# A two-block fp32 model on one core: unit 0 of the second scan prepared between the value tiles of the shift projection

## What is computed

```python
cols = cols + (bidir_shift(cols) - cols) * mu          # 0.5 * (left + right neighbour)
r, k, v, w_lo, a_lo, g_lo = split(cols)                # widths 512, 512, 512, 128, 128, 128
w_log = -softplus(-(w0 + tanh(w_lo) @ w2)) - 0.5
decay = exp(-exp(w_log))
iclr = sigmoid(a0 + a_lo @ a2)
kk = l2norm(heads(k * k_k))
k_dir = heads(k * (1 + (iclr - 1) * k_a))
b_dir = kk * heads(iclr)
y = rwkv7_scan(r, decay, k_dir, v, -kk, b_dir)         # two directions, 8 heads of 64
...
y = sigmoid(g_a) * (o_a @ w_o_a) + sigmoid(g_b) * (o_b @ w_o_b)
```

## Time and profile before

| | |
|---|---|
| time of the kernel, median of 3 runs | 2380.62 us (2380.04 to 2385.37) |
| the profiled execution's own time | 2382.07 us |
| its span | 2380.3 us |
| mean granted PE clock | 0.985 |
| PE busy | 2265.9 us, 95% |
| DVE, ACT, POOL busy | 1189.4, 1003.6, 300.1 us |
| shift projection, end of its last matmul | about 1804.3 us |
| unit 0's products begin on PE | 1816.76 us |
| second half of unit 0's base begins on PE | 1821.71 us |

### The profile page before, as it was taken

How to read it: one execution, slowest core, us unless ns; L and a number is a source line. 1 busy time by engine, 2 the same in 40 slices (tenths; PEclk the granted TensorE clock), 3 DMA queues, 4 the chain that set the end, 5 groups by cost and what they waited for, 6 DMA issues and landing times.

```text
span 2380.3 us, 51755 instructions
## 1 busy us (share of the span) xinstructions
PE 2265.9 (95%) x23025; PEld 1905.8 (80%) x23025; DVE 1189.4 (50%) x2080; ACT 1003.6 (42%) x1614; POOL 300.1 (13%) x421
## 2 busy tenths in 40 slices
PE   7999999999999999999999999998999898899877
PEld 7999887889999999887889999568846787786432
DVE  5655544276655665544266655755453445432101
ACT  5434456444434444457445434643225544312111
POOL 0100000040100110000040100026312333300000
PEclk9999999999999999999999999999999999999988
DMA  8754532256655754532346762320112102087998
GB/s 269 248 204 169 169 137 101 94 179 196 228 195 177 248 204 168 199 112 102 107 159 205 244 211 88 106 73 4 42 36 72 39 8 70 8 338 278 420 421 336
DMA packets 209679, 396.61 MB, mean 167 GB/s; under 512 B 9512, under 2 KB 107613, under 8 KB 198573
## 3 DMA queue, kind: packets, MB, share of 16 engines
q1 hardware_dynamic: 207273, 388.79, 46.0%
q0 software_dynamic: 1136, 2.17, 0.3%
q10 hardware_dynamic: 1044, 2.29, 0.3%
HBM read 392.18 MB, written 1.05 MB: 165 GB/s over the span
## 4 chain that ended last, share of the span: by engine, by line
PE 85%; DVE 4%; DMA 4%; SPq 3%; ACT 2%; issue 2%; POOL 0%; ACTq 0%; DVEq 0%; POOLq 0%
PE ps L286 84%; DMA EX<-in_moe_w_up 3%; SPq L454 2%; SPq L560 1%; PE ps L1196 0%; DVE wl L487 0%; DVE AR L699 0%; ACT AR L2962 0%; ACT AR L2954 0%; DVE AR L2017 0%; PE ps L583 0%; ACT AT L1250 0%; DMA VR<-in_diff_gain 0%; DVE AR L1778 0%; ACT wh L478 0%
## 5 line engine op out<-in xcount | busy, mean ns | idle before, releaser
L487 DVE TENSOR_TENSOR wl<-RB,wh 128x2048 fp32r<-128x2048 f32 (+5 forms) x189 | 412.3, 2185 | 273.2 <-ACT wh L478 272.8
L286 PE MATMUL ps<-H,RB 128*128 128x256 f32 (+2 forms) x1728 | 452.8, 421 | 2.5 <-ACT AR L2933 1.3
L478 ACT ACTIVATE wh<-RB 128x2048 fp32r<-128x2048 f32 (+5 forms) x189 | 342.2, 1815 | 226.1 <-PE ps L286 200.0
L286 PEld LDWEIGHTS ps<-H,RB 128*128 128x128 f32 (+1 forms) x1728 | 320.2, 190 | 114.2 <-issue 76.2
L286 PE MATMUL ps<-xhf,wl 128*128 128x256 f32 x1408 | 402.3, 286 | 3.3 <-DVE xlf L728 2.4
L286 PE MATMUL ps<-xlf,wh 128*128 128x256 f32 x1408 | 398.8, 283 | 0.0
L286 PE MATMUL ps<-xhf,wh 128*128 128x256 f32 x1408 | 398.8, 283 | 0.0
L286 PE MATMUL ps<-AR 64*64 64x64 f32 (+6 forms) x8536 | 278.5, 233 | 40.3 <-issue 22.2
L286 PEld LDWEIGHTS ps<-AR 64*64 64x64 f32 (+3 forms) x8536 | 252.7, 142 | 75.3 <-issue 56.9
L286 PEld LDWEIGHTS ps<-xhf,wl 128*128 128x128 f32 x1408 | 270.6, 192 | 14.5 <-issue 9.4
L286 PEld LDWEIGHTS ps<-xlf,wh 128*128 128x128 f32 x1408 | 270.8, 192 | 0.1
(11 more groups left out here) (444 smaller groups left out, 3371.7 us busy)
## 6 DMA issues: line engine op xcount, KB each, us to landing
RB<-in_ffn_w_gu SPq DMA_DIRECT2D x88, 1024.0 KB, 7.7
RB<-in_w_in SPq DMA_DIRECT2D x23, 2048.0 KB, 8.0
RB<-in_ffn_w_down SPq DMA_DIRECT2D x16, 2048.0 KB, 7.8
RB<-in_w_gate SPq DMA_DIRECT2D x16, 2048.0 KB, 8.7
RB<-in_ada_w SPq DMA_DIRECT2D x12, 2048.0 KB, 10.1
EX<-in_moe_w_gate SPq DMA_DIRECT2D x21, 1024.0 KB, 23.3
EX<-in_moe_w_up SPq DMA_DIRECT2D x21, 1024.0 KB, 25.7
EX<-in_moe_w_down SPq DMA_DIRECT2D x9, 2048.0 KB, 25.9
```

Source lines behind the costliest of these rows:

```text
L286: return M.matmul(o, lhsT, rhs, start=start, stop=stop, skip_group_check=True)
L478: S.activation(self.pair(h)[0], of(slot_of(*key)), ACT.Copy).then_inc(*did("high", *mark))
L487: V.tensor_tensor(lo, of(slot_of(*key)), hi.bitcast(F32), ALU.subtract).then_inc(*did("low", *mark))
```

## The change

It changes seven things, all around the shift projection and the list of the scan:

- The tiles run in the order 0 to 7, 12, 13, 14, 8, 9, 10, 11 (`tiles`), and the low-rank weights are loaded ahead of the value's.
- Behind the places 10 to 13 (`early`) each engine walks the pieces of unit 0's preparation and its products. `scan_pe` and its kin take the list as an argument, and are called with `ahead(p)`.
- `PAD` and `SX` lie in a buffer of their own (`SPARE`), as their old place belongs to unit 0's preparation. The expert slot that shares this memory waits for `moved 11` instead of an earlier mark.
- Unit 0 reads the small weights straight from `EARLY`. The copies into `HB` stand behind the last tile, and POOL waits for all three (`g2`, `a2`, `w2`) before it begins the scan's list.
- From place 9 on the tiles use banks 0 to 3, the turns of the value tiles bank 4, each one place later against its tile; the last stands behind the last tile. The first branch's output is turned behind place 8.
- `merge0` 0 and 1 stand between `base_a` and `base_b` of slot -1, both in bank 4.
- `gate0` 0 moves from the old front into slot -1, 1 into its end, and 2 into slot 0. Slot -1 keeps two gates, slot 0 has gates 2 and 3; from slot 1 on the list is as before. `weigh` 0 and 1 follow them.

The core of the diff:

```diff
-        for i in range(4):
+        for i in (0, 1, 3, 2):
             job(("rkv", i), ...
...
-            order = prepared(0, 0, 1) + fill(("merge0", 0, 0)) + prepared(0, 2) + fill(*gate(0), ("merge0", 1, 0))
-            order += prepared(0, *range(3, 7)) + [(("products", 0, o),) for o in range(2)] + fill(("weigh", 0, 0))
-            sigmoid = {-1: gate(1), 3: [("merge0", 6, 0)] + gate(6)}
+            order = []
+            sigmoid = {-1: gate(0), 0: gate(2), 3: [("merge0", 6, 0)] + gate(6)}
...
-            end = {i: gate(i + 3) for i in range(-1, 3)}
+            end = {i: gate(i + 3) for i in range(3)}
+            end[-1] = gate(1)
...
-                slot = [solve(n, "base_a", 0), solve(n, "base_b", 0)] + prepared(p, 0)
+                slot = [solve(n, "base_a", 0)] + fill(*([("merge0", 0, 0), ("merge0", 1, 0)] if i < 0 else []))
+                slot += [solve(n, "base_b", 0)] + prepared(p, 0)
...
+            tiles = (*range(8), 12, 13, 14, *range(8, 12))
+            early = {10: [("prep", 0, 0)], 11: [("prep", 0, 1), ("prep", 0, 2)], 12: [("prep", 0, x) for x in (3, 4, 6)],
+                     13: [("products", 0, 0), ("products", 0, 1)]}
...
+                        ps = bank(("shift", n), ("shift_pad", n), among=every_bank if p < 9 else (0, 1, 2, 3))
...
-                    if 9 <= n < 13:
-                        vj = n - 9
+                    if p < 15:
+                        scan_pe(ahead(p))
+                    if p >= 12:
+                        vj = p - 12
                         PE.wait_ge(*at("moved", 8 + vj))
-                        ps = bank(("turned", "rv", vj), ("rv_rows", vj))
+                        ps = bank(("turned", "rv", vj), ("rv_rows", vj), among=(4,))
...
+                PO.wait_ge(*upto("low_rank"))
+                PO.wait_ge(*at("shift", 11))
+                P.tensor_copy(G2, EARLY[2]).then_inc(*did("g2"))
+                PO.wait_ge(*at("g2"))
+                PO.wait_ge(*at("a2"))
+                PO.wait_ge(*at("w2"))
```

More of the change, by code:

```diff
@@ L2529, in rwkv, with ahead @@
             BON = SM[:, 1248:1264].rearrange("p (k c) -> p k c", k=4)
-            PAD = [area(10496 + 516 * i, 516).rearrange("p (s n) -> p s n", s=2) for i in (1, 2, 0)]
-            SX = [area(15616 + 512 * i, 2, T) for i in (1, 2, 0)]
+            spare = sb("SPARE", O_SPARE, [3084])
+            PAD = [view(spare, 516 * i, 2, 258) for i in range(3)]
+            SX = [view(spare, 1548 + 512 * i, 2, T) for i in range(3)]
+            tiles = (*range(8), 12, 13, 14, *range(8, 12))
+            early = {10: [("prep", 0, 0)], 11: [("prep", 0, 1), ("prep", 0, 2)], 12: [("prep", 0, x) for x in (3, 4, 6)],
+                     13: [("products", 0, 0), ("products", 0, 1)]}
+            def ahead(p):
+                return [(piece,) for piece in early.get(p, ())]
             VTT, KKS, KKR = (area(x, 2, 512) for x in (17664, 19712, 21760))
@@ L2549, in shift_pe @@
             def shift_pe():
[L2550 to L2553, removed]
+                for p in range(16):
+                    tail_pe(p)
+                    if p < 15:
+                        n = tiles[p]
+                        i, j = divmod(n, 4)
                         nc_ = 512 if i < 3 else 384
@@ L2589, in shift_act @@
                 AC.wait_ge(*at("shift_zero", 2))
[L2590 to L2599, removed]
+                for p in range(16):
+                    tail_act(p)
+                    if 5 <= p < 9:
+                        kj = p - 5
                         AC.wait_ge(*at("kk_in", kj))
@@ L2603, in shift_act @@
                         S.activation(KKS[:, kj % 2, :], KKT[:, kj, :], ACT.Square).then_inc(*did("squared", "kk", kj))
-                    if n == 9:
+                    if p == 9:
                         AC.wait_ge(*at("turned", "o", 1))
[L2606 to L2610, removed]
+                        for q in range(2):
+                            S.activation(OAT.rearrange("p (c e) n -> p e c n", e=2)[:, q], ps_of("turned", "o", q).rearrange(
+                                "p (c n) -> p c n", c=2), ACT.Copy).then_inc(*did("o_rows", q))
+                    if p >= 13:
+                        vj = p - 13
                         AC.wait_ge(*at("turned", "rv", vj))
@@ L2637, in shift_dve @@
                 ins.then_inc(*did("blk"))
-                for n in range(15):
-                    tail_dve(n)
+                for p in range(15):
+                    tail_dve(p)
+                    n = tiles[p]
                     i, j = divmod(n, 4)
-                    if n == 13:
-                        DV.wait_ge(*upto("low_rank"))
-                        DV.wait_ge(*at("shift", 13))
-                        V.tensor_copy(A2, EARLY[1])
-                        V.tensor_copy(W2[1], EARLY[3]).then_inc(*did("a2"))
-                    if 6 <= n < 10:
-                        kj = n - 6
+                    if 6 <= p < 10:
+                        kj = p - 6
                         root_dve(f"kk{kj}", KKR[:, kj % 2, :])
@@ L2677, in shift_dve @@
                                 *did("kk_in", j))
+                    scan_dve(ahead(p))
+                DV.wait_ge(*upto("low_rank"))
+                DV.wait_ge(*at("shift", 11))
+                V.tensor_copy(A2, EARLY[1])
+                V.tensor_copy(W2[1], EARLY[3]).then_inc(*did("a2"))
             def shift_pool():
@@ L2765, in pairs_pe @@
                     PE.wait_ge(*at("o_rows", 1))
-                    ps = bank(("merge", 0, i), ("yb", 0, i), among=kept if i > 1 else (3, 4))
+                    ps = bank(("merge", 0, i), ("yb", 0, i), among=kept)
                     for k in range(4):
@@ L2773, in pairs_pe @@
                         PE.wait_ge(*landed("mgate", 0, i // 4))
-                        bank(("mgate", 0, i), ("mgated", 0, i), among=kept if i else (3, 4))
+                        bank(("mgate", 0, i), ("mgated", 0, i), among=kept)
                     ps = ps_of("mgate", 0, i)
@@ L2782, in pairs_pe @@
                 elif what == "prep" and x == 0:
[L2783 to L2784 removed]
+                    PE.wait_ge(*at("low_act", 12))
+                    if i:
+                        PE.wait_ge(*at("w2"))
+                        PE.wait_ge(*at("a2"))
+                    else:
+                        PE.wait_ge(*upto("low_rank"))
                     ps = bank(("w_in", i), ("w_sig", i), among=others)
[L2786 removed]
+                    mm(ps[:, :], TWD[u.dr][:, u.ts], W2[u.dr] if i else EARLY[0], True, True).then_inc(*did("w_in", i))
                 elif what == "prep" and x == 1:
@@ L3111, in scan_pool @@
                             v.level_pool(x)
-            scan_pe()
-            scan_act()
-            scan_dve()
-            scan_pool()
+            shift_pool()
+            scan_pool(order)
+            shift_pe()
+            scan_pe(order)
+            shift_act()
+            scan_act(order)
+            shift_dve()
+            scan_dve(order)
             return merge(area, Y0, SG1, gate1_pe, gate1_act)
```

84 lines of the change are left out of this document (42 added, 42 removed).

## The result

| | before | after |
|---|---|---|
| median | 2380.52 us (2376.98 to 2385.37, 20 runs) | 2387.17 us (2384.25 to 2395.22, 20 runs) |
| ratio, 95% interval | | 1.003 (1.0023 to 1.0036) |
| span of the profiled execution | 2380.3 us | 2385.3 us |

What follows compares the result with a forecast made beforehand. TensorE, busy for 95% of the span, was taken to bound the kernel. Front, full clock and slot 0 summed as -2.0 - 1.5 + 1.8 = -1.7 us, giving a forecast median of 2379.0 us, with a range of 2374.5 to 2384.5.

Steps and rivals of the forecast that it cites:

- The four waits: Front: new PE waits at the products' fourth bank 1.9, last turn 2.7, merge's first piece 0.65 and second 0.5 us.
- -1.5 more: Behind the base's second half: full clock saves 0.5 us on the base and 1.05 on unit 1's first matmul.
- rival 2: Front, last turn to merge: low clock comes back, costing 3.0 us on merge matmuls; 2381.9 us, chance 0.30.
- The relay: Last turn: tile 11 moves over ACT, POOL and DVE; 3.4 + 0.37 - 1.1 = 2.7 us of wait.
- the old stretch: Front of the kernel before: PE at 1.2 instead of 2.4 GHz from about 1818.5 to 1824.9 us.
- ACT's table loads included: Unit 0's preparation: costed at no wait, three tiles of 7.1 us covering what took 12.5 us, table loads included.
- 1.05 us less: Slot -1: unit 1's first matmul at full clock, 1.02 us against 2.07.
- Slot 0: A second gate between adaptation and level 2 costs 1.8 us, taken between 1.25 and 2.4; at most 3.65.
- The relief of the issue wait: Slot 0: dense gate work lets the instruction stream catch up, removing a later 1.15 us wait; cost then 1.25.
- rival 1: Only the idle PE is filled, the stream not relieved: 2.4 us in slot 0; 2379.6 us, chance 0.12.
- The list of what would show it: Changed profile: tiles 7.1 us apart, waits 1.9 and 2.7, base's second half at about 62, slot 0 gate stretch 5.8.
- Rival 3: Under tile 11: the fourth bank's wait drops the clock, +3.2 us; 2382.2 us alone, chance 0.10.

Runs made afterwards that it cites:

- e3_turn: Changed kernel with the fourth value tile's turn issued in slot -1 behind the second merge piece instead of ahead of the base: 2379.81 us, ratio 0.9999.
- e5_fill: Changed kernel with five more matmuls that nothing reads, two ahead of the products' fourth bank, three ahead of the last turn: 2383.16 us, ratio 1.0011.
- c7_all: Second measurement of the changed kernel with early table load, fourth bank from free banks, last turn in slot -1, merge's first piece in another bank: 2375.22 us, ratio 0.9982.
- e6_gate: Changed kernel with the gate pieces one place earlier, as in the kernel before (one in the front, none in slot 0): 2388.61 us, ratio 1.0036.
- e8_order: Changed kernel's tile order and padded-tile scratch, but unit 0's preparation, merge and gates as in the kernel before: 2383.85 us, ratio 1.0022.
- c6_after: Changed kernel, unchanged, profiled again for its first 85 us: 2390.17 us, measured one time.
- e1_table: Changed kernel with one small sigmoid on ScalarE behind unit 0's preparation, loading the sigmoid's table under the value tiles: 2385.49 us, ratio 1.0022.
- c1_after: Changed kernel, unchanged, measured again beside the kernel before: 2386.13 us, ratio 1.003.
- e2_bank: Changed kernel with the fourth bank of unit 0's products taken from the banks of the solving: 2383.55 us, ratio 1.0014.
- e4_all: First measurement of the changed kernel with early table load, fourth bank from free banks, last turn in slot -1, merge's first piece in another bank: 2377.25 us, ratio 0.9988.

## Why the prediction was wrong, point by point

For the three stretches of the sum the forecast was 83.0 (85.5 - 2.0 - 0.5), 27.7 (28.7 - 1.05) and 30.2 us (28.4 + 1.8).

**The account of the front was right, its clock was not.** The four waits came out at 2.17, 2.68, 0.79 and 0.47 where the text had 1.9, 2.7, 0.65 and 0.5. At full clock the front would have taken 85.7 less 0.8 on the last turn and 1.8 on merge's piece, 83.1 us. The low clock, "-1.5 more" in the sum, was the step that failed, in two ways. It came back, which was rival 2, and at its price: 2.6 to 2.8 us shown by e3_turn and e5_fill, 3.0 in the text. (The relay was priced rightly too: DVE's step took 1.06 us at 1813.01, beside POOL's copy.) I gave it 0.30 where three of three executions have it. The argument against it was one idle spell of 1.95 us that left the clock alone. And the 1.5 us that the old stretch cost was no property of the kernel before: four of its five profiles have a front of 84.5 us, and only the one that I read has 85.5. So 1.0 us of the forecast gain was taken off a draw. The working has a small slip beside it: 0.53 in the microsecond from 1818 puts the fall at 1818.06 and not at 1818.5, so the products lost 0.56 us by it (2.64 against 2.08 in c7_all) and not 0.4; and it did not see that the wait of 0.25 us grows to 0.69 when the clock stays full.

**The preparation was not free behind itself.** "ACT's table loads included" looked at loads inside the preparation. It missed that the gate moved out of the front had loaded the sigmoid's table for slot -1: 0.92 us on PE. The rest of the slot's loss is smaller and in part open. The three executions of the changed kernel take 29.7 to 30.3 us and have 0.52, 0.68 and 1.07 us of issue waits; the kernel before, in its three executions at full clock there, takes 27.7 to 28.5 and has 0.52, 0 and 0.36. So of some 1.8 us, 0.9 is the table, about 0.5 the issue waits, and 0.4 nothing that the rows name. Why the issue waits are more was not tested; the sum had none of this and counted on 1.05 us less, the clock's share on unit 1's first matmul, which was part of the same draw.

**Slot 0 was under-priced.** 1.8 was a middle between 1.25 and 3.65; the account said 2.4, and 2.4 was measured (5.84 against 3.40 us in the trace; in e6_gate and e8_order, which have no second gate there, the slot is 2.6 and 2.4 us shorter). The relief of the issue wait did not come: 1.09, 0.82 and 1.40 us in three executions, after 0.88 to 1.43 in five of the kernel before. On that number rival 1 was right, and with it the sum by the Trainium skill's page (Runtime: NRT & Kernel Launch, section Instruction fetch mechanics). Whether its reason, that fetching is hidden, holds here no run shows: the issue waits stand in every execution, and nothing names their cause.

**Outside the sum:** slot 1 is 0.8 us longer on average, with a low stretch in two of three profiles that the kernel before lacks; and the stretch up to the root, 1.3 us, of which 1.0 arises in the first 85 us, which no step of mine looked at.

By stage, from the forecast, which stands on the execution of the rows, to the mean of after: front 3.2 (2.6 of it one low stretch, 0.5 a second one in c6_after), slot -1 2.3, slot 0 0.6, slot 1 0.5, start 1.9, rest -1.5. That is 7.0 of the 7.1 us from a forecast span of 2378.6 to 2385.7. The other 1.1 of the 8.2 us between the forecast 2379.0 and the median 2387.2 lie in how far the profiled executions stand above their medians: 1.4 us was taken off for it in the forecast, and it is 0.3 for the three of the changed kernel. The steps that failed are thus, by size, the clock in the front (2.6 us) and the two slots behind it: the sum booked -1.05 and +1.8 us for them, and they are 1.4 and 2.4 us longer than the kernel before's.

The list of what would show it served: tiles 7.1 us apart and the two waits were as said, the base's second half was 64.5 us behind the third key sum instead of 62, and the granted clock near 0.50 before 1820 named rival 2. The range failed because it let rivals 2 and 3 fill it and left no room for two or three unpriced losses of 1 us each on top. Rival 3 deserved more than 0.10: of the six executions that have the wait of 2.17 us in the products, c6_after, e1_table and e6_gate have the low stretch under tile 11, at 1.5 to 1.7 us each and not 3.2. And the measurement was finer than the 0.3% that the text allowed it: its interval, 1.0023 to 1.0036, lies clear of 1.

## What to carry to other kernels

Do not book a low-clock stretch of one profile as a cost of the kernel: read it in several executions before taking it off. When work moves out of a stretch, ask what it did besides its product: here it had loaded ACT's table. A tile whose result must pass three engines is best not the last one; two more pieces between it and its consumer were worth 5.5 us, half of it through the clock.

## What the runs showed of the hardware

- A dense tile, 1.1 us of 64x64 matmuls, an idle of 2.67 or 2.68 us and 64x64 matmuls again went with a fall to 1.2 GHz in seven of seven executions (after, c1_after, c6_after, e1_table, e2_bank, e6_gate, e8_order). With the idle filled or gone, the clock fell in none of four (e3_turn, e5_fill, e4_all, c7_all). An idle of 2.17 us at the end of the products went with a fall in three of six, and the one of 1.97 us in the kernel before in one of five.
- From 100 to 1500 us all seventeen profiled executions run in lockstep: offsets between them change by less than 0.2 us. Up to there they differ by what arises in the first 85 us, where a stretch of low clock costs 1.4 to 2.7 us.
- Issue waits inside dense 64x64 matmuls differ between executions of one kernel: in slot -1 they add up to 0.52, 0.68 and 1.07 us in the changed kernel, and to 0 to 0.52 in the kernel before. No cause is shown.
- A load of ACT's table took 1.28 us and moved with the work: without the gate in the front it stood in slot -1 and held PE for 0.92 us; a sigmoid of one column under the tiles took that wait away (e1_table).
- The same 128x512 step of DVE took 0.69 us by itself, 1.06 beside POOL's copy of `g2` and 1.74 beside POOL's product for unit 0 (changed kernel, 1783.4, 1813.0 and 1792.5 us; the same in its two other profiles).
